# Ranking a tile's experts in two halves of 64 tokens, in a two-block transformer kernel with a product-key expert layer

## The reference, cut to what matters

```python
def chunk(hc):                                    # 128 tokens, width 1024
    q = (hc @ w_query).reshape(128, 8, 2, 64)      # 8 heads, 2 parts
    s = jnp.einsum('chpd,hpnd->chpn', q, sub_keys) # 128 keys per head and part
    s_top, i_top = lax.top_k(s, 16)
    cand = (s_top[:, :, 0, :, None] + s_top[:, :, 1, None, :]).reshape(128, 8, 256)
    cand_id = (i_top[:, :, 0, :, None] * 128 + i_top[:, :, 1, None, :]).reshape(128, 8, 256)
    best, pos = lax.top_k(cand, 16)
    eid = jnp.take_along_axis(cand_id, pos, axis=-1)
    gate = jax.nn.softmax(best, axis=-1)
    u = jnp.take(u_tab, eid, axis=0)               # 128 rows of 1024 floats for each token
    act = jax.nn.gelu(jnp.einsum('chkd,cd->chk', u, hc)) * gate
    v = jnp.take(v_tab, eid, axis=0)               # and 128 more
    return jnp.einsum('chk,chkd->cd', act, v)
```

## Time and profile before

| | |
|---|---|
| median of 3 runs | 3523.64 us (3520.84 to 3527.73) |
| span of the profiled execution, first to last instruction | 3317.3 us |
| median less that span | 206.3 us |
| PE busy | 2336.2 us, 70% of the span |
| DVE busy | 1679.4 us, 51% |
| POOL busy | 1480.8 us, 45% |
| ACT busy | 558.5 us, 17% |
| moved by DMA | 1047.22 MB, 880.90 of it by POOL's gathers |

### The profile page before, as it was taken

How to read it: one execution, slowest core, us unless ns; L and a number is a source line. 1 busy time by engine, 2 the same in 40 slices (tenths; PEclk the granted TensorE clock), 3 DMA queues, 4 the chain that set the end, 5 groups by cost and what they waited for, 6 DMA issues and landing times.

```text
span 3317.3 us, 36982 instructions
## 1 busy us (share of the span) xinstructions
PE 2336.2 (70%) x12540; PEld 1281.0 (39%) x12540; DVE 1679.4 (51%) x4368; ACT 558.5 (17%) x1179; POOL 1480.8 (45%) x1577
## 2 busy tenths in 40 slices
PE   7899867898999888995465444447898545444444
PEld 5477624365777545764121000004587400000000
DVE  2521576644233586436965444443712795444444
ACT  2320231401100235102240000002511210000000
POOL 1100044444444444430666777771000167777775
PEclk9999978799999898997575555557899755555555
DMA  8967679899999896991999999993233299999998
GB/s 307 352 209 267 238 269 350 304 354 378 362 365 366 323 347 235 363 334 64 375 349 388 409 409 409 409 409 111 70 114 134 84 379 409 409 409 406 409 409 341
DMA packets 325915, 1047.22 MB, mean 316 GB/s; under 512 B 27424, under 2 KB 38752, under 8 KB 325728
## 3 DMA queue, kind: packets, MB, share of 16 engines
q0 software_dynamic: 240192, 880.90, 69.2%
q1 hardware_dynamic: 85536, 163.95, 14.1%
HBM read 1043.70 MB, written 1.05 MB: 315 GB/s over the span
## 4 chain that ended last, share of the span: by engine, by line
PE 49%; DVE 18%; issue 13%; DMA 10%; ACT 3%; PEld 3%; POOL 2%; PEldq 0%; DVEq 0%; ACTq 0%; POOLq 0%
PE ps L404 24%; PE ps L440 12%; DVE UV L1044 8%; DMA UV<-in_v_tab,idxT 7%; PE ps L426 4%; PEld ps L404 3%; ACT arena L1679 2%; PE ps L396 2%; DMA W<-in_w_mod 2%; POOL UV L2157 1%; PE ps L529 1%; PE ps L571 1%; DVE arena L1415 1%; DVE arena L1424 1%; DVE arena L1418 1%
## 5 line engine op out<-in xcount | busy, mean ns | idle before, releaser
L1044 DVE SCALAR_TENSOR_TENSOR UV<-ps,UV 128x1024 f32<-128x1024 f32 x768 | 909.8, 1222 | 833.4 <-PE ps L426 816.3
L2157 POOL DMA_INDIRECT UV<-in_u_tab,idxT x768 | 723.5, 942 | 1182.4 <-DVEq L1510 498.1
L440 PE MATMUL ps<-UV,acts 128*32 128x512 f32 x3072 | 632.5, 908 | 560.3 <-DVE acts L1053 456.6
L2167 POOL DMA_INDIRECT UV<-in_v_tab,idxT x768 | 724.9, 944 | 281.6 <-issue 198.8
L404 PE MATMUL ps<-H,W 128*128 128x256 f32 (+2 forms) x3296 | 668.7, 363 | 36.4 <-ACT H L1679 26.5
L404 PEld LDWEIGHTS ps<-H,W 128*128 128x128 f32 (+1 forms) x3296 | 574.7, 194 | 147.3 <-issue 76.6
L404 PE MATMUL ps<-arena,W 128*128 128x256 f32 (+1 forms) x1632 | 371.6, 385 | 20.4 <-issue 8.6
L440 PEld LDWEIGHTS ps<-UV,acts 128*32 128x32 f32 x3072 | 78.3, 129 | 716.1 <-DVE acts L1053 572.7
L404 PEld LDWEIGHTS ps<-arena,W 128*128 128x128 f32 (+1 forms) x1632 | 304.4, 190 | 103.3 <-issue 53.2
L426 PE MATMUL ps<-hs,selb 32*128 32x512 bf16 x1536 | 208.5, 530 | 153.1 <-DVE UV L1044 153.0
L1679 ACT ACTIVATE gel<-dots 128x2 f32<-128x2 f32 x384 | 77.4, 202 | 1255.9 <-DVE UV L1044 1247.3
(11 more groups left out here) (198 smaller groups left out, 1698.9 us busy)
## 6 DMA issues: line engine op xcount, KB each, us to landing
W<-in_w_in SPq DMA_DIRECT2D x30, 2048.0 KB, 10.1
UV<-in_w_mod POOLq DMA_DIRECT2D x18, 2048.0 KB, 12.3
W<-in_w_ff SPq DMA_DIRECT2D x16, 2048.0 KB, 14.2
UV<-in_w_ada POOLq DMA_DIRECT2D x9, 2048.0 KB, 11.7
W<-in_w_out SPq DMA_DIRECT2D x8, 2048.0 KB, 11.4
W<-in_w_mod POOLq DMA_DIRECT2D x6, 2048.0 KB, 19.9
W<-in_w_query SPq DMA_DIRECT2D x6, 2048.0 KB, 9.2
UV<-in_u_tab,idxT POOLq DMA_INDIRECT x768, 8.8
```

The source lines that it names most:

```text
L440: last = mm(ps[q:q + GROUP, YB, :], acts[:, tok % SLOTS, GROUP - 1 - r:2 * GROUP - 1 - r], Vs[:, tok % SLOTS, hf * 512:(hf + 1) * 512], st ...
L1044: dve.scalar_tensor_tensor(out=Us[:, j, :], in0=ps[:, b:b + 2, :].rearrange("p a b -> p (a b)"), scalar=1.0, in1=Us[:, j, :], op0=MUL, op1 ...
L2157: pool.indirect_dma_start(Us[:, j, :], None, A["u_tab"], off).then_inc(sem(f"u_arrived{j}"), 16)
L2167: pool.indirect_dma_start(Vs[:, j, :], None, A["v_tab"], off).then_inc(sem(f"v_arrived{j}"), 16)
```

## The change: the first tiles of x are ranked in two halves of 64 tokens

Tiles 2 and 4 (`SPLIT`) are now ranked in two parts of 64 tokens. Within a part the 128 partitions hold 64 tokens twice: the lower 64 partitions hold heads 0, 1, 4, 5 and the upper 64 hold heads 2, 3, 6, 7 (by the index rule in `scores`), so that a part has 8 rows of scores instead of 16, and 4 rows of candidates instead of 8. A part has the steps `top 0`, `top 1`, `pairs 0`, `pairs 1`, `keys 0` to `keys 3`; each `top` and each `pairs` step is as long as before, and each `keys` step works on half the elements. The four transposes of a part are matmuls with a 64 by 64 identity. `idx_ready` is raised for each part, and POOL waits at pair 0 and at pair 32 of such a tile. The second part is ranked at the start of `route_second`, with visits of the first part's pairs between its steps, ahead of the second tile's scores. Tiles 0, 1, 3 and 5 are ranked as before. Lines have moved down: PE's L404, L823, L839, L840, L802, L426, L440 of before are L417, L836 (L844 for the split tiles), L868 and L869, L815, L439, L453; DVE's L1412 to L1424, L1429, L1438, L1507 and L1044 are L1447 to L1459, L1465, L1474, L1553 and L1079.

```diff
+HALF = P // 2
+SPLIT = (2, 4)
+def parts(n):
+    return 2 if n in SPLIT else 1
+def part_no(n, r):
+    return sum(parts(m) for m in range(n)) + r
+def steps_of(n):
+    tops = 4 // parts(n)
+    return [f"top {e}" for e in range(tops)] + [f"pairs {e}" for e in range(tops)] + [f"keys {e}" for e in range(4)]
...
-                while owed[0] >= PACE and seen[0] < min(segment[1], PAIRS * ready[0]):
+                while owed[0] >= PACE and seen[0] < min(segment[1], ready[0]):
...
+                for i in range(4 if parts(n) == 2 else 0):
+                    for b in range(2):
+                        h, at = 4 * a + 2 * b + i % 2, n % 2 * P + i // 2 * HALF
+                        for p in range(2):
+                            last = mm(o[p][HALF * b:HALF * b + HALF, i * P:(i + 1) * P], qp[64 * p:64 * p + 64, h, at:at + HALF],
+                                      keys[64 * p:64 * p + 64, h, :], start=True, stop=True)
...
+                for step in steps_of(n):
+                    top = step.startswith("top")
+                    beat((step, n, r), (4.4 if top else 3.2) if n == 1 else 12.4 if top else 7.6)
...
+                    f = slice(HALF * r, HALF * r + HALF)
+                    for b in range(2):
+                        q = slice(HALF * b, HALF * b + HALF)
+                        mm(o[q, 0:HALF], eid[q, f], ident[q, q], start=True, stop=True)
+                        last = mm(o[q, HALF:P], g[q, f], ident[q, q], start=True, stop=True)
...
-                ready[0] = n + 1
-                ready_at[n] = seen[0]
+                ready[0] = PAIRS * n + PAIRS * (r + 1) // parts(n)
+                ready_at[n, r] = seen[0]
...
             def route_second(tag, beside={}):
 
                 n = TILE_OF[tag] + 1
+                rows_by_pair(n - 1, [0])
+                if parts(n - 1) == 2:
+                    routes(n - 1, 1, {"top 0": [lambda: rows_by_pair(n - 1, range(1, 8))]})
                 for a in range(2):
-                    rows_by_pair(n - 1, [a])
                     scores(n, a)
...
-                    dve.wait_ge(sem("scores_ready"), 4 * n + 2 * (e // 2 + 1))
-                    sixteen_best(top, tix, sc, [(i, i) for i in range(4 * e, 4 * e + 4)])
+                    dve.wait_ge(sem("scores_ready"), 4 * n + 2 * (e // 2 + 1 if parts(n) == 1 else e + 1))
+                    sixteen_best(top, tix, sc, [(i, i) for i in range(8 * r + 4 * e, 8 * r + 4 * e + 4)])
...
-                    sixteen_best(best, pos, cand, [(2 * e + i, 2 * e + i) for i in range(2)])
+                    sixteen_best(best, pos, cand, [(4 * r + 2 * e + i, 4 * r + 2 * e + i) for i in range(2)])
...
+                        act.wait_ge(sem("ranked"), no)
+                        i = slice(2 * nh * r, 2 * nh * (r + 1))
+                        A_(tixe[:, i, :, :], tixb[:, i, :].unsqueeze(3).to_broadcast([P, 2 * nh, TOPK, TOPK])).then_inc(sem("ranks_spread"), 1)
...
-                if 2 * g % P == 0:
-                    pool.wait_ge(sem("idx_ready"), 2 * g // P + 1)
+                n = g // PAIRS
+                r = g % PAIRS * parts(n) // PAIRS
+                if part_at[n, r] == g:
+                    pool.wait_ge(sem("idx_ready"), part_no(n, r) + 1)
```

More of the change, by code:

```diff
@@ L819, in scores @@
                 o = [bank(("sc", n, a, p)) for p in range(2)]
-                for hh in range(4):
+                for hh in range(4 if parts(n) == 1 else 0):
                     h = 4 * a + hh
@@ L844, in route_first @@
+                full(last, ("ij", n, r))
+                ready[0] = PAIRS * n + PAIRS * (r + 1) // parts(n)
+                ready_at[n, r] = seen[0]
             def route_first(tag):
@@ L1434, in sum_ranks @@
-            def sum_ranks(a):
+                flat = part.rearrange("p h r s -> p h (r s)")
+                link(dve.tensor_tensor(out=flat, in0=flat, in1=f4[:, hh, a, :], op=MUL))
+            def sum_ranks(a, hh):
                 for r in (8, 4, 2, 1):
[L1437 to L1451, removed]
-                    dve.tensor_tensor(out=hp3, in0=hres, in1=hp2, op=SUB).then_inc(sem("parts_ready"), 1)
-                elif what == "top":
-                    dve.wait_ge(sem("scores_ready"), 4 * n + 2 * (e // 2 + 1))
-                    sixteen_best(top, tix, sc, [(i, i) for i in range(4 * e, 4 * e + 4)])
-                    if e == 3:
-                        dve.tensor_copy(tixb, tix).then_inc(sem("ranked"), 1)
@@ new lines, in route @@
+            def route(n, r, step):
+                what, e = step.split()[0], int(step.split()[-1])
+                nh, no = PH // parts(n), part_no(n, r) + 1
+                hh, f = slice(nh * r, nh * r + nh), slice(16 * nh * r, 16 * nh * (r + 1))
+                lasts = 4 // parts(n) - 1
+                if what == "top":
+                    dve.wait_ge(sem("scores_ready"), 4 * n + 2 * (e // 2 + 1 if parts(n) == 1 else e + 1))
+                    sixteen_best(top, tix, sc, [(i, i) for i in range(8 * r + 4 * e, 8 * r + 4 * e + 4)])
+                    if e == lasts:
+                        two = slice(2 * hh.start, 2 * hh.stop)
+                        dve.tensor_copy(tixb[:, two, :], tix[:, two, :]).then_inc(sem("ranked"), 1)
@@ L1512, in hidden @@
-            def hidden(n):
-                route(n, "residue")
-                route(n, "parts")
-            def routes(n, at, beside={}):
-                for step in STEPS[at:-1]:
-                    route(n, step)
-                    beat(step, n)
+                        link(dve.scalar_tensor_tensor(out=eid[:, f], in0=ij[:, 0, hh, :].rearrange("p a b -> p (a b)"), scalar=float(NKEY),
+                                                      in1=ij[:, 1, hh, :].rearrange("p a b -> p (a b)"), op0=MUL, op1=ADD))
@@ L1522, in routes @@
+            def routes(n, r, beside={}):
+                for step in steps_of(n):
+                    route(n, r, step)
+                    beat(step, n, r)
                     if n == 0:
@@ L1546, in route_second @@
                     beat("tile 1 done")
-                routes(n, 2, beside)
+                routes(n, 0, beside)
                 if tag != "c0":
```

167 lines of the change are left out of this document (97 added, 70 removed).

## The result

The changed kernel takes 3502.22 us (median of 4 runs) against 3525.68 us of the kernel before in the same series: ratio 0.9934, 95% interval 0.9917 to 0.9951, so 23.5 us faster by the medians and 17 to 29 us by the interval. The forecast was 3502.0 us, 21.6 us faster.

What follows compares the result with a forecast made beforehand. Gathers bound each stream of visits; two ranking stretches before them have no visit beside. 28.0 - 5.7 - 5.7 + 5.0 = 21.6 us off 3317.3 gives 3295.7, plus 206.3 makes 3502.0 us; range of 8 in 10: 3488 to 3517.

Steps and rivals of the forecast that it cites:

- The start: Ranking ahead of tiles 2 and 4: first gather 35.4 us plus twice the extra score time after the first `top`, from 50.0.
- The price d: Extra time of a split tile's scores on PE from doubled matmul instructions: taken 0.3 us, bounds 0 and 1.16.
- What the stream gives back: Second half's 27.2 us of ranking beside eleven visits on a full DVE: 5.7 us lost at each place.
- The stall that goes: Start of layer 1's stream: DVE's 5.10 us wait for tile 5's scores goes, returning 5 us.
- The sign named for it: Over the first 185 us of each stream, GB/s lower than 409 by about 15 us' worth in either layer.
- the 0.21 us of each: Loss per us of ranking beside visits, at most, taken from tile 5's 47 us; no row can show it.
- the 14 that the prediction named as a sign of being wrong: POOL's gaps beside the second half adding up to 14 us would show the forecast wrong.
- Slower: Rival, chance 0.08: second half not hidden, all 27.2 us paid, each place 13 us worse, 3545 us.
- Small gain: Rival, chance 0.20: streams give back 11.4 us at each place, score price 1.16; 6.8 us gained, 3517.
- all comes back: Rival, chance 0.08: 14 us lost at each place in the streams; about 3519 us, within 0.2%.
- large gain: Rival, chance 0.12: visits beside the second half swallow all its ranking, scores cost nothing extra; 34 us gained, 3489.
- With the 206.3 us around it: Constant taken from the median as time outside the span, added to the predicted span of 3295.7 for 3502.0 us.

Runs made afterwards that it cites:

- both again: The changed kernel unedited, timed again in another series at 409 GB/s: 3298.94 us against 3322.92 for the kernel before, ratio 0.9922.
- x0: The changed kernel with only tile 2 (layer 0) split: 3542.87 us, ratio 0.9986 to the kernel before; in a later series 3520.6 us, 0.9981.
- x1: The changed kernel with only tile 4 (layer 1) split: 3543.36 us, ratio 0.9985 to the kernel before; in a later series 3522.49 us, 0.999.
- the kernel before, again: The unedited kernel before, run once more for a trace in the session of the experiments: 3555.2 us, span 3553.4.

## Why the prediction was right, step by step

- **The start.** Forecast 35.4 + 2d us from the first `top` step to the first gather, measured 35.15 at both places. The second `top` step begins at 9.34 (9.34 + 2d), `keys` at 26.48 (26.5 + 2d), the 64-wide operation takes 0.22 us (0.223 by the slope), the table copy 1.91 (1.9), the sums of each table 1.27 us (1.80 less 0.5). The gain at each place is 14.86 us where 14.0 was taken.
- **The price d.** Taken 0.3, bounds 0 and 1.16. The 32 matmuls of a query take 1.10 us where 16 took 1.16, so d is 0 or a little below, where PE's wait ahead of them is 0.80 us in both. That fits matmuls of two row groups and two column groups running side by side. The nearest row, L440 of the earlier trace rows, pointed that way. No extra time is to be seen at the change of shape either: the next query matmuls begin 1.03 us behind the first score matmul (1543.65), where they began 1.09 us behind it before. The Trainium skill (TensorEngine Tiling (Array Packing), Key Properties) says that tiles work in parallel, with which the trace agrees, and that a change of mode drains the engine. No row shows the drain by itself; the shape changes here before as after, so a cost of it would be in both.
- **What the stream gives back.** At 409 GB/s, from tile 2's first gather to tile 4's: 1060.65 us before, 1051.57 in "both again", which has tile 4's start 14.86 us sooner. 1051.57 + 14.86 - 1060.65 = 5.8 us are given back in layer 0; the forecast was 5.7. In layer 1, from the first gather to the end of the span: 690.7 against 689.4 us, 1.3 us given back where the forecast had 5.7 - 5.0 = 0.7. The stall that goes is there to be read: the first dot comes 8.8 us behind the first gather (2615.19) and not 13.9. Where in the stream the 5.8 us of layer 0 lie isn't shown. The sign named for it, GB/s below 409 worth about 15 us over the first 185 us, came as 366 and 372 GB/s, 19.5 and 16.7 us; before, the same stretches have 356 and 376, 24.0 and 14.9 us. So that sign can't tell the second half's price from the other work of the stretch.
- **The sum.** In layer 0 9.1 us (8.3 forecast), in layer 1 13.6 (13.3), together 22.7 where 21.6 was forecast; these are from one trace each, and 24.0 was timed in that series. That the sizes agree so closely at each of five terms is some luck, above all for the 0.21 us of each that no row could show. The forecast of the split between layers can't be told from the timed runs, where x0 and x1 alone gave much the same. At the slow rate, at which the result was timed, the traces have it the other way round: 16 to 20 us for layer 0 and 8 to 14 for layer 1, so layer 0 gives nothing back and layer 1 some of its 14.9. That the total came out at that rate too is then partly luck, for the terms of the stream were not those of the forecast.
- **The waits and rivals.** No gap at pair 32 (2779.07 above, 0.30 us). POOL's gaps beside the second half are 1.71 and 2.47 us in layer 1 and 2.67 and 3.56 in layer 0, and 4.60 at tile 5's first scores: far from 14 at this rate. In the slow trace of the changed kernel the gaps over 1 us there add up to 20.2 and 17.9 us, past the 14 that the prediction named as a sign of being wrong. But the kernel before has 20.9 and 19.5 us of them in the same first 78.6 us of its streams at that rate ("the kernel before, again"): they come with the rate and not with the second half. The sign had been set from a trace at 409 GB/s and doesn't hold at another rate. "Slower" needed the visits to stand still, and the experiment without them shows that it would have happened at this very place. The stretch between the streams changed by little, as forecast: POOL's wait for tile 4 is 356.55 us where it was 369.93, 13.4 us less, to which the split gave 14.9, so the rest grew by 1.5 us. "Small gain", "all comes back" and "large gain" each needed another give-back than the 5.8 and 1.3 of the traces. The gather waited for nothing but the list.
- **What was wrong: "With the 206.3 us around it".** The difference between the median and the span of before isn't time around the span, which is 1.8 us. It is gathers at 355 to 365 GB/s in the timed runs and 409 in the trace. The predicted time came out because the same 206 us were added to both; the gain had been summed from stretches in which no gather runs and from a give-back at the fast rate. That step was wrong, and the time came out all the same: had the gain hung on the gathers' rate, it would have been off. At the slow rate POOL's gaps are also larger (7.69 us at 1601.73 in the changed kernel, against 3.56 at 1596.81 in "both again"), and the two places together gained 23.5 and 17.8 us.

## What to carry to other kernels

Where a stream waits for a list that is made in steps, measure the distance from the first step to the first transfer: half the list is worth that distance less what the halves cost more, provided that work stands beside the other half (here 14.9 us gained at each place and 16 us lost in all when it didn't). When one wait is removed, name what is late next and move that too: the 2.4 us wait for ACT's copy, read off the old timeline, was worth another 4.4 us of time. And before adding a constant "around the span" to a forecast, check that the rate of the bound resource in the trace fits the timed runs.

## What the hardware showed that I had not expected

- The rate of the 4 KB-row gathers differs between series of the same kernel, on different chips where the chip is known: 409 GB/s with a DMA share of 1.03 in one, 362 with 0.96 in another, in stretches where nothing else is moved; the whole program took 3323 or 3525 to 3549 us. Stretches without gathers agree to 0.03 us (50.00 to 50.03 from `top` to the first gather).
- 32 float32 matmul rows of the trace (two for each instruction), 64 rows by 64 output columns and 128 wide, took 1.10 us; 16 of 64 by 128 took 1.16. With the freed output half used, doubling the instructions cost nothing.
- At about 355 GB/s two changes that act 1.1 ms apart gave 17.8 and 23.5 us together and 9.3 and 12.5 us as the sum of the parts, in different series; the cause isn't known.
